# Where six expert turns and the gate broadcast stand in a hand-written order: two layers of a hybrid diffusion backbone on one core

## What is computed

```python
for l in range(DEPTH):                       # DEPTH = 2; context (yp) and latent (ys) both
    mix = token_mix(y * (1 + sc1) + sh1)     # projections, attention, Fourier mix, output projection
    y = layer_norm(ALPHA * y + g1 * mix, ln1_g[l], ln1_b[l])
    y = layer_norm(ALPHA * y + g2 * peer_ffn(y * (1 + sc2) + sh2), ln2_g[l], ln2_b[l])

def peer_ffn(h):                             # 16384 single-neuron experts, top 16 for each of 8 heads
    ...                                      # pick 128 experts e and gates g for each token
    a = einsum('tkd,td->tk', u_tab[e], x)
    w = g * gelu(a)
    return einsum('tk,tkd->td', w, v_tab[e])
```

## Time and profile before

| what | value |
|---|---|
| median of 3 runs | 2656.72 us (2655.41 to 2671.84) |
| the profiled execution | 2653.2 us |
| its span, first to last instruction | 2651.4 us |
| TensorE matmuls busy | 2167.9 us, 82% of the span |
| VectorE busy | 1526.2 us, 58% |
| ScalarE, GpSimd busy | 687.8 us, 931.3 us |
| mean granted clock of TensorE | 0.924 of full speed |
| moved by DMA | 961.92 MB, mean 363 GB/s |
| of it gathered expert rows | 805.36 MB |

### The profile page before, as it was taken

The page is one execution under the profiler, slowest core; times in us unless marked ns, Lnnn a source line. Parts: engine busy times, 40 slices in busy tenths (PEclk is TensorE's granted clock), DMA queues, the critical chain, the costliest instruction groups (busy, mean ns, idle before and its releaser), DMA issues.

```text
span 2651.4 us, 25198 instructions
## 1 busy us (share of the span) xinstructions
PE 2167.9 (82%) x7370; PEld 1175.1 (44%) x7370; DVE 1526.2 (58%) x3555; ACT 687.8 (26%) x1864; POOL 931.3 (35%) x868
## 2 busy tenths in 40 slices
PE   7988899989677788898778799999877776777775
PEld 5676554566233344354443465467533332222222
DVE  0164566456888645545668355645877766555554
ACT  2332365221211122332112235522121111211111
POOL 0001234223344443343335123322343443455652
PEclk9987999999788899899898899999988898999998
DMA  9966999789799999999999699979889999999996
GB/s 398 417 233 274 332 355 381 286 334 369 298 387 388 377 421 409 400 374 410 395 419 358 244 337 344 393 280 362 337 307 410 394 390 368 399 405 422 422 422 263
DMA packets 142619, 961.92 MB, mean 363 GB/s; under 512 B 15920, under 2 KB 24240, under 8 KB 28208
## 3 DMA queue, kind: packets, MB, share of 16 engines
q0 software_dynamic: 110592, 805.36, 76.3%
q1 hardware_dynamic: 30912, 152.06, 14.8%
q10 hardware_dynamic: 1008, 3.17, 0.3%
HBM read 958.17 MB, written 2.36 MB: 362 GB/s over the span
## 4 chain that ended last, share of the span: by engine, by line
PE 42%; DMA 26%; DVE 15%; issue 8%; ACT 5%; POOL 3%; SPq 1%; POOLq 0%; DVEq 0%; ACTq 0%
DMA uv_rows<-in_peer_uv,index 24%; PE acc L737 21%; PE pair L800 7%; PE pair L859 5%; POOL uv_rows L610 3%; DVE products L1262 2%; PE pair L764 2%; DMA wtiles<-in_w_in 1%; PE pair L837 1%; DVE arena L1182 1%; PE pair L680 1%; ACT arena L907 1%; ACT L907 1%; ACT diag L927 1%; PE pair L658 1%
## 5 line engine op out<-in xcount | busy, mean ns | idle before, releaser
L737 PE MATMUL acc<-uv_rows,diag 128*128 128x512 f32 x3072 | 1474.7, 632 | 344.3 <-ACT diag L927 344.3
L610 POOL DMA_INDIRECT uv_rows<-in_peer_uv,index x768 | 890.0, 1159 | 1462.0 <-PE acc L737 1305.0
L1262 DVE CUSTOM_DVE_ANT_0 products<-uv_rows,h_tok 128x1024 bf16<-128x1024 f32 x768 | 942.1, 1227 | 588.9 <-DMA uv_rows<-in_peer_uv,index 582.2
L737 PEld LDWEIGHTS acc<-uv_rows,diag 128*128 128x128 f32 x3072 | 601.4, 202 | 1159.3 <-issue 666.0
L927 ACT ACTIVATE diag<-consts,weight 128x128 f32<-128x128 f32 x768 | 266.1, 395 | 372.6 <-DVE weight L1252 372.6
L932 ACT ACTIVATE gelu<-dots 128x2 f32<-128x2 f32 x384 | 77.8, 203 | 1039.5 <-DVE dots L1262 1039.1
L800 PE MATMUL pair<-wtiles,hT 128*128 128x256 f32 x976 | 223.7, 388 | 16.5 <-DMA wtiles<-in_w_in 8.3
L800 PEld LDWEIGHTS pair<-wtiles,hT 128*128 128x128 f32 x976 | 190.6, 196 | 57.6 <-issue 22.7
L1252 DVE TENSOR_TENSOR weight<-gelu,gates 128x2 f32<-128x2 f32 x384 | 61.9, 161 | 200.7 <-ACT gelu L932 197.0
L878 ACT COPY arena<-pair 128x256 f32<-128x256 f32 (+3 forms) x154 | 84.5, 553 | 324.1 <-PE pair L859 129.2
L859 PE MATMUL pair<-hT,wtiles 128*128 128x256 f32 (+1 forms) x864 | 154.2, 337 | 0.0
(11 more groups left out here) (114 smaller groups left out, 1186.7 us busy)
## 6 DMA issues: line engine op xcount, KB each, us to landing
uv_rows<-in_w_mod SPq DMA_DIRECT2D x36, 1024.0 KB, 15.0
wtiles<-in_peer_wq SPq DMA_DIRECT2D x27, 1024.0 KB, 6.9
wtiles<-in_w_in SPq DMA_DIRECT2D x24, 1024.0 KB, 10.0
wtiles<-in_w_out SPq DMA_DIRECT2D x15, 1024.0 KB, 7.7
wtiles<-in_w_mod SPq DMA_DIRECT2D x12, 1024.0 KB, 14.0
uv_rows<-in_peer_uv,index POOLq DMA_INDIRECT x768, 10.0
rows<-in_ln_g SPq DMA_DIRECT2D x12, 512.0 KB, 9.3
rows<-in_ln_b SPq DMA_DIRECT2D x12, 512.0 KB, 12.6
```

What stands on the lines that cost most here:

```text
L610: pool.indirect_dma_start(out=uv_rows[:, slot, :], out_offset=None, in_=i["peer_uv"], in_offset=bass.IndirectOffsetOnAxis(ap=index[:, half ...
L737: last = nc.tensor.matmul(acc[:, n, :], diag[:, g, j, :], uv_rows[:, slot, D + n * 512:D + (n + 1) * 512], start=False, stop=True, skip_gr ...
L1262: nc.vector.tensor_tensor_reduce(out=products[:, :], in0=uv_rows[:, slot, 0:D], in1=h_tok[:, slot_q, :], scale=1.0, scalar=0.0, op0=ALU.mu ...
```

## The change

Two edits in `beside`. Block 3 loses its own start: it now opens as the others do, with turns 0 to 5 around the two halves of the layer norm, and mix 3's steps begin after turn place 6 and not 2. And gate2 of every block goes in front of all the turns that are left when the steps are through, and no longer in front of the last two places.

```diff
     if q:
         out = [("gather", q, 0, 2), ("ln2", q - 1, 0), ("gather", q, 2, 4), ("ln2", q - 1, 1), ("gather", q, 4, 6)]
         at = 6
-        if q == BLOCKS[2][0]:
-            out = [("gather", q, 0, 1), ("ln2", q - 1, 0), ("gather", q, 1, 2), ("ln2", q - 1, 1)]
-            at = 2
     ahead = at
...
-    late = max(at, TURNS - 2)
-    return out + [("gather", q, at, late)] * (at < late) + [("gate2", q), ("gather", q, late, TURNS)]
+    return out + [("gate2", q), ("gather", q, at, TURNS)]
```

## The result

The changed kernel takes 2701.93 us (median of 4 runs, 2695.21 to 2705.81), the kernel before beside it 2663.94 (4 runs): a ratio of 1.0141, 95% interval 1.0093 to 1.0188. It is slower, by 1.4%, and by more than the range of the prediction allowed. The profiled execution after took 2704.75 us with a span of 2702.9; against the profiled one of before that is 51.6 us more.

A forecast was written before the change was run, and what follows sets the result against it. No single bound: transfers set the pace in block 5, TensorE in mix 3's queries. Terms -7.2 + 2 + 2 + 1 + 1 + 0 - 1 - 1 = -3.2 took 2653.2 to 2650.0; adjusted for the runs' median, forecast 2653 us, range 2635 to 2678.

The forecast's parts named there:

- place 6: Opening of block 5: gate2 there delays turn 4's slots, +2 us, bounds 0 and +4; TensorE's spare then catches up.
- At the next seam the removal of the broadcast takes most of that back: Seam after block 4: rows some 6 us late, but 7.2 us saved before the drain; bounds -1.2 and +6.
- behind pick 5 of block 5: In block 4, turn 49 stands behind the broadcast, turn 54's rows come some 6 us late; net +2 us.
- behind pick 5 in blocks 0 and 3: Turn 58 runs behind the broadcast; slots 13 us late catch up by turn 63: +1 us each, bounds -1 and +6.
- In block 1 gate2 passes one turn and waits on no pick: 0: End of block 1: moving gate2 costs nothing, 0 us, bounds -2 and +2.
- the end: After block 5's last dot: without gate2's broadcast there the drain comes earlier, -7.2 us, bounds -6.5 and -7.5.
- Rival (a): Ring left dry behind pick 5 in blocks 0, 2, 3, 4, 6 us lost each: +21, 2678 us; chance 0.18.
- the opening of block 3: A wait for rows replaces the layer norm wait, 29.9 to 32.1 us drain to gelu and modulation: -1 us.
- The prediction's own test: Wrong if the drain after block 3 or 4 comes over 6 us later, or block 3 gets over 10 us shorter.
- block 2: −1: Block 2, behind pick 5 of block 3: rows some 6 us late, 7.2 us saved before the drain; bounds -2 and +6.
- (b): Seam to block 3: empty DMA was the price, the seam gives 21 us; -25 in all, 2632 us; chance 0.08.
- (c): Seam to block 3: filling TensorE's gap gives 15 us, kernel at 2639 us; chance 0.12.

The follow-up runs named there:

- gates alone: Against the kernel before, only gate2 moves as in the change, block 3 keeps its old start: 2688.60 us, ratio 1.0087.
- one turn first: Against the changed kernel, TensorE's broadcast and ScalarE's copy one place later at the picks of blocks 0, 2, 3, 4: 2677.92 us, 1.0058 to the kernel before.
- drain first: Against the changed kernel, the layer norm's first half goes ahead of turns 0 and 1 at every seam: 2684.53 us, 1.0092 to the kernel before.
- both: The changed kernel with the edits of one turn first and drain first together: 2661.60 us, 0.9998 to the kernel before.
- the opening alone: Against the kernel before, only block 3's opening is changed, gate2 stays at place 64: 2668.24 us, ratio 1.0003.
- place 40: Against the kernel before, block 5's gate2 alone moves, unsplit, to place 40: 2661.04 us, ratio 1.0003.
- the split versions: Against the kernel before, gate2 cut in three spread steps, in block 5 alone (2659.93 us, 0.9982) or blocks 4 and 5 (2656.26 us, 0.9968).
- the split last block: Against the kernel before, block 5's gate2 alone is split over places 40, 44 and 48: 2659.93 us, ratio 0.9982.

## Why the prediction was wrong

The steps of the lag, us, for the runs that tell causes apart. "Unchanged" is the range of the same step in all runs whose code there is that of before.

| place | change | gates alone | one turn first | drain first | both | unchanged |
|---|---|---|---|---|---|---|
| end of block 0 | +11.1 | +9.8 | +5.9 | +6.2 | +1.9 | +0.3 to +3.3 |
| end of block 1 | +7.7 | +8.3 | +8.1 | −1.0 | −0.8 | −1.1 to +0.6 |
| end of block 2, opening | +10.4 | +1.1 | +5.0 | +6.1 | +1.4 | −0.8 to +0.8 |
| end of block 3 | +9.8 | +11.0 | +6.0 | +7.4 | +2.5 | −0.4 to +1.5 |
| end of block 4 | +9.9 | +8.8 | +4.0 | +4.8 | −1.9 | −0.4 to +1.5 |
| place 6 | +2.9 | +2.2 | +1.5 | +2.2 | +3.2 | −0.1 to +1.4 |

At block 1's end some of the step goes back later in block 2 in two runs (to its turn 50: gates alone +2.9, one turn first +2.0 remain; change +7.3). Unchanged code has −2.2 to +3.8 up to there, so a price of block 1 that stays shows in the change alone.

**The step that failed** is "At the next seam the removal of the broadcast takes most of that back", and with it the size of four terms: behind pick 5 of block 5 +2 (measured +9.9), behind pick 5 in blocks 0 and 3 +1 each (+11.1, of which unchanged code has up to 3.3, and +9.8), and "In block 1 gate2 passes one turn and waits on no pick: 0" (+7.7). The prediction named the order on which it turns, that the drain "stands on VectorE behind the dots of two more turns, whose rows are the late ones", and then took the lateness to be smaller than the 7.2 us saved. But those rows need not even be late. At the pace of the transfers the four dots ahead of the drain fill all but 1.0 to 2.6 us of what the seams behind blocks 0, 2, 3 and 4 took before, and at every seam TensorE idles 6.5 to 9.4 us ahead of the clearing, with turn 63 done. What shows it is the drain put first: the seams behind blocks 0, 3 and 4 then give back 1.6 to 3.4 us in the lag where they added 1.1 to 2.0, with the holds themselves in place, and on top of the other cure it is worth 16 us.

**The hold is lost by itself too.** It was sized at 6 us and meant to be hidden. Behind a pick the dots fall 9 to 11 us behind, and 5 to 9 us of it are left at turn 63, before the seam comes. In block 4 it is 8.8 us (46.0 to 54.8), and with the DMA share at 1.01 behind it that stays so. One turn of TensorE inside the pick is what separates the kernels: putting it back takes 22 us off. These two prices add, and with both gone the change is neutral, 0.9998: within that interval, 6 us either way, they are the whole loss, and the rest cancels (the end's −7.3 against place 6's +3.2 and small steps).

**Rival (a)** described this ("the holds are not taken back") and its deciding point came true at every seam. It was given 0.18, and at +21 it was too small: it counted 6 us a pick and no loss in block 1 or at the opening of block 3. The prediction's own test fired as well: block 3, drain to drain, takes 500.8 us against 488, block 4 361.7 against 348, both over the 6 us that were to make it wrong.

**The opening of block 3.** The chain was right (31.2 us predicted between 29.9 and 32.1; 28.75 in the opening alone), and so was its own worth of about zero (−1 predicted, 1.0003 measured, an interval that the +4.0 of its lag lies within). But of the 16.8 us of work that was to be saved behind it, the copies of the projections show less: in the opening alone their lag rises by 14 at the first and falls by 10 over the mix. And "block 2: −1" holds only with the old opening, which has one turn ahead of the drain; with the new one block 2's hold is kept, +10.4. That is where both edits together step by more than the two alone. Where in mix 3 the missing 7 us went was not followed.

**Right:** the end (−7.2 predicted, −7.3 in every run without gate2 there), and the size of place 6 (+2 within 0 to +4; +2.9 and +3.2, of which unchanged code has up to 1.4). The dots did not catch up behind it, though (15.6 at turn 16, 15.7 at turn 63), and place 40 shows that the same hold costs more, +5.8, where the ring is in steady pace.

**Rivals (b) and (c).** The stretch without transfers at the seam is gone in the opening alone (DMA share of the 30 us from the drain 0.95, before 0.39), and the TensorE gap of 9.54 and 3.20 us is replaced by one of 8.11, and neither moved the time. The Trainium skill ("Perfetto Trace Analysis", section "Optimization Strategies") advises to clear what makes the matmul engine wait if it lies on the critical path. The opening alone shows how much hangs on that condition: TensorE waits 4.6 us less there, and the time shows no gain. At the picks TensorE's own wait does cost, through the slots that it doesn't free.

```profile
1476.00:1506.00 30.00, 17.27 (x60) 12.06 (x59) 15.05 (x25) 9.24 (x25) 2.10 (x4) 0.72 0.39 145
```

```profile
1482.00:1512.00 30.00, 20.50 (x56) 9.72 (x55) 20.30 (x35) 10.55 (x30) 13.90 (x12) 0.85 0.95 384
```

## What to carry to other kernels

Where transfers are issued by what an engine frees, as in this ring, a step put ahead of the last ready turn costs the ring's empty time, and in the stretches at full DMA share here that time did not return. Before moving a step up, count the turns that were running inside the wait it will stand behind, and split it so that each engine does its share when the input lies ready. A saving at a seam is worth only the distance to what is late next. Look for what stands ahead of the seam's first instruction on its own engine, and ask whether the same edit makes just that late. Two edits can meet at such a place, as at the end of block 2, so try them apart and together.

## What was not expected of the hardware

In all runs together, gate2's broadcast took 3.34 to 3.76 us behind a wait of TensorE of 6.4 us or more, in most of them 3.75, and 1.88 us where it follows a turn directly (the split versions). The granted clock goes with it: 0.50 in the first row, the lower of TensorE's two levels (1.2 of 1.2 and 2.4 GHz), behind 15.53 us of idle time, against 1.00 in the last row, where the turn ahead had waited 1.3 us. The turns that follow a cold broadcast run at 0.94 in the mean, so the lower clock costs this step 1.9 us and what stands behind it little. First after (broadcast of block 4, then the four turns), then the split last block:

```profile
2286.50:2290.00 3.50, 3.50 (x5) 1.42 (x6) 2.23 (x4) 0.00 (x0) 0.00 (x0) 0.50 0.02 5
2290.00:2304.00 14.00, 14.00 (x32) 6.15 (x31) 4.39 (x9) 3.29 (x9) 5.87 (x7) 0.94 0.63 219
```

```profile
2545.50:2547.50 2.00, 2.00 (x6) 0.95 (x5) 0.93 (x4) 0.90 (x3) 1.19 (x2) 1.00 1.05 438
```
